# Softmax q/k group norm and short convolution placed inside the first input projection

## The reference, cut to what matters

```python
h = rmsnorm(x, attn_norm_w[l])
proj = h @ w_in[l]                     # 1024 -> 3072 columns
(q_a, k_a, v_a, q_b, k_b, v_b, g_b, g_c, x_c) = jnp.split(proj, split_points, axis=-1)
y_sb = from_heads(stick_breaking_attention(to_heads(q_a), to_heads(k_a), to_heads(v_a)))
qh = rmsnorm(to_heads(q_b), q_norm_w[l])   # per head of 64 features
kh = rmsnorm(to_heads(k_b), k_norm_w[l])
y_ch = from_heads(chunked_relpos_attention(qh, kh, to_heads(v_b), rel_bias[l]))
y_cv = short_conv_mixer(g_b, g_c, x_c, conv_w[l])  # gate * causal conv of width 3
y = group_rmsnorm(jnp.concatenate([y_sb, y_ch, y_cv], axis=-1), out_norm_w[l])
x = x + y @ w_out[l]
```

## Time and profile before

| | |
|---|---|
| device time, median of 3 runs | 2940.41 us (2938.57 to 2943.82) |
| device time of the profiled execution | 2938.94 us |
| its span in the trace | 2937.1 us |
| TensorE busy | 2767.3 us, 94% of the span |
| VectorE busy | 1657.0 us, 56% |
| GpSimd busy | 1157.6 us, 39% |
| ScalarE busy | 841.9 us, 29% |
| mean granted TensorE clock | 0.977 of full speed |

### The profile page before, as it was taken

One profiled execution on the slowest core, in us unless ns is written; L12 is line 12 of the kernel. 1 busy time (PEld: TensorE's weight loads), 2 busy tenths in 40 slices (PEclk: granted clock), 3 DMA queues, 4 the chain that ended last, 5 costly groups with the idle time before them and its releaser, 6 DMA issues.

```text
span 2937.1 us, 38574 instructions
## 1 busy us (share of the span) xinstructions
PE 2767.3 (94%) x13164; PEld 2188.6 (75%) x13164; DVE 1657.0 (56%) x3297; ACT 841.9 (29%) x1285; POOL 1157.6 (39%) x976
## 2 busy tenths in 40 slices
PE   6997899999999987999999999999999999999997
PEld 5863478878788764778777777888888888888775
DVE  4135642111599537469999956444444444444787
ACT  1133323322222427123445521222222222222111
POOL 4410155555455430453410044444444444444442
PEclk9988999999999999999999999999999999999998
DMA  4210033323223220222346764443443443443442
GB/s 141 88 36 22 15 94 95 98 93 100 87 93 94 78 88 28 65 89 79 94 151 236 253 196 140 114 129 113 115 129 110 119 128 109 120 124 112 128 129 64
DMA packets 208200, 315.44 MB, mean 107 GB/s; under 512 B 139888, under 2 KB 142320, under 8 KB 203888
## 3 DMA queue, kind: packets, MB, share of 16 engines
q1 hardware_dynamic: 63792, 233.34, 25.5%
q10 hardware_dynamic: 144320, 80.94, 10.0%
HBM read 275.45 MB, written 38.80 MB: 107 GB/s over the span
## 4 chain that ended last, share of the span: by engine, by line
PE 43%; issue 23%; DVE 18%; POOL 14%; ACT 1%; DMA 0%; DVEq 0%; ACTq 0%; POOLq 0%
POOL lo L431 14%; PE bank L1247 14%; PE bank L1248 14%; PE bank L1249 14%; DVE ohg L1173 3%; DVE bank L1200 1%; DVE oh L1169 1%; DVE oh L1170 1%; DVE WH L1202 1%; DVE lo L1181 1%; DVE eq L1146 1%; DVE idx L1088 1%; DVE idx L1080 1%; DVE scb L1081 1%; PE bank L1364 1%
## 5 line engine op out<-in xcount | busy, mean ns | idle before, releaser
L431 POOL TENSOR_TENSOR lo<-raw,hi 128x256 fp32r<-128x256 f32 (+1 forms) x972 | 1157.4, 1218 | 1741.5 <-ACT hi L457 911.9
L1247 PE MATMUL bank<-inH,hi 128*128 128x512 f32 x2240 | 893.9, 399 | 28.4 <-DVE inL L798 15.9
L1248 PE MATMUL bank<-inL,hi 128*128 128x512 f32 x2240 | 879.9, 393 | 0.0
L1249 PE MATMUL bank<-inH,lo 128*128 128x512 f32 x2240 | 879.6, 393 | 0.0
L1208 DVE TENSOR_TENSOR xT<-xT,bank 128x512 f32<-128x512 f32 x504 | 339.6, 685 | 538.4 <-PE bank L1249 538.4
L1247 PEld LDWEIGHTS bank<-inH,hi 128*128 128x128 f32 x2240 | 425.6, 190 | 125.9 <-issue 32.9
L1249 PEld LDWEIGHTS bank<-inH,lo 128*128 128x128 f32 x2240 | 425.0, 190 | 90.7
L1248 PEld LDWEIGHTS bank<-inL,hi 128*128 128x128 f32 x2240 | 426.2, 190 | 88.1 <-issue 2.2
L1247 PE MATMUL bank<-WH,hi 128*128 128x512 f32 x1024 | 408.5, 399 | 14.9 <-DVE xT L1208 14.9
L1248 PE MATMUL bank<-WL,hi 128*128 128x512 f32 x1024 | 404.0, 395 | 0.0
L1249 PE MATMUL bank<-WH,lo 128*128 128x512 f32 x1024 | 400.5, 391 | 0.0
(11 more groups left out here) (205 smaller groups left out, 2430.3 us busy)
## 6 DMA issues: line engine op xcount, KB each, us to landing
raw<-stream SPq DMA_DIRECT2D x440, 512.0 KB, 3.6
Gd<-gates ACTq DMA_DIRECT2D x32, 1024.0 KB, 7.4
gates<-stage_a ACTq DMA_DIRECT2D x16, 1024.0 KB, 4.3
gates<-stage_b ACTq DMA_DIRECT2D x16, 1024.0 KB, 4.2
tbl<-gqa ACTq DMA_DIRECT2D x8, 384.0 KB, 3.3
spilled<-res ACTq DMA_DIRECT2D x12, 256.0 KB, 3.1
A<-spilled ACTq DMA_DIRECT2D x6, 512.0 KB, 3.7
xT<-x SPq DMA_DIRECT2D x1, 2048.0 KB, 8.8
```

Of the source, the lines that this page charges most:

```text
L431: ins = pool.tensor_tensor(lo[:, r, part], raw[:, r, part], hi[:, r, part].bitcast(F32), ALU.subtract)
L1247: pe.matmul(bank, wh, xh, start=start, stop=False)
L1248: pe.matmul(bank, wh, xl, start=False, stop=False)
L1249: return pe.matmul(bank, wl, xh, start=False, stop=stop_)
```

## The change: what it does, and the diff

The norm of q_b and k_b and the convolution move ahead of stick-breaking attention, into the 24 tiles of the projection. VectorE squares tile m right after it took tile m out of its bank (m = 4 to 11). TensorE makes the sum of tile m-6 after tile m (m = 6 to 13); its loop over tiles 4 to 15 is written out for that. ScalarE takes the root in its turn of tile 15, and its loop is written out too. VectorE's reciprocal follows its copy of tile 15. TensorE spreads the first two tiles' roots after tile 17 and the other six after the first and third token group of each value pair (t = 0 and t = 2). VectorE's multiplications and the two halves of the convolution stand around its copies of the value tiles. Softmax attention then follows stick-breaking attention directly; ScalarE starts the loads of `tbl1b` right after its last copy there.

```diff
 # ScalarE
-            with act.Fori(1, N_IN // RING) as i:
-                for r in range(RING):
-                    high(S_IN, i, r + AHEAD)
+            for m in range(RING, N_IN):
+                if m == ROOT_TILE:
+                    group_root(n_sums + KD)
+                    n_sums += KD
+                high(S_IN, 0, m + AHEAD)
...
-            group_root(n_sums + KD)
-            n_sums += KD
             table(stage1, 1)
             attention(stage1)
 # VectorE
+            for m in range(18):
+                evacuate(m)
+                if 4 <= m < 12:
+                    square_qk(m - 4)
+                if m == ROOT_TILE:
+                    group_roots(n_root + 1)
+            put_qk(0)
+            put_qk(1)
+            dve.wait_ge(evac, T_IN + 18)
+            short_conv(0)
+            put_qk(2)
+            short_conv(1)
+            put_qk(3)
+            for m in (18, 20):
+                evacuate(m)
+                evacuate(m + 1)
+                put_qk(m // 2 * 2 - 14)
+                put_qk(m // 2 * 2 - 13)
             dve.wait_ge(spread_used, KD)
             dve.sem_inc(in_ready, 1)
+            evacuate(22)
+            evacuate(23)
 # TensorE
-            linear(S_IN, T_IN, 16, 1)
-            for m in (16, 17):
+            for m in range(RING, 18):
                 pe.wait_ge(evac, m - RING + 1)
                 pe.wait_ge(lo_done, m + 1)
                 tile(m % RING, B[m % RING][:, :])
+                if 0 <= m - SUM_LAG < KD:
+                    group_sum(n_sq, m - SUM_LAG)
+            n_sq += KD
+            n_rt += 1
+            pe.wait_ge(recips, n_rt)
+            spread_group(0, 0)
+            spread_group(1, 0)
             for m in range(18, N_IN, 2):
-                tiles_by_token(S_IN, T_IN, m)
+                tiles_by_token(S_IN, T_IN, m, lambda part: spread_group(m - 16 + part, 0))
+            pe.wait_ge(in_ready, 2)
...
             pe.wait_ge(y_sb, 2)
-            n_rt += 1
-            group_norm(n_sq, n_rt, 0, KD)
-            n_sq += KD
-            pe.wait_ge(in_ready, 2)
             attention(stage1)
```

More of the change, by code:

```diff
@@ L110 @@
 N_GRPS = D // HD
+SUM_LAG = 6
+ROOT_TILE = SUM_LAG + KD + 1
 PARTS = 2
@@ L831, in over_root, with group_roots @@
                 dve.reciprocal(rr[:, :width], rr[:, :width]).then_inc(recips, 1)
+            def group_roots(nth_root):
+                dve.wait_ge(roots, nth_root)
+                dve.reciprocal(rt[:N_GRPS, 0, :], rt[:N_GRPS, 0, :]).then_inc(recips, 1)
             def group_norm(src, put, n, nth_root, n_spread):
                 square_sums(src, n)
-                dve.wait_ge(roots, nth_root)
-                dve.reciprocal(rt[:N_GRPS, 0, :], rt[:N_GRPS, 0, :]).then_inc(recips, 1)
+                group_roots(nth_root)
                 for k in range(KD):
@@ L894, in _, with evacuate @@
             n_root += 1
-            for m in range(N_IN):
+            def evacuate(m):
                 dve.wait_ge(slot_used, S_IN + m + 1)
@@ L904, in _, with square_qk, put_qk, short_conv @@
                     take(m, dve.tensor_copy(by_token(v1, m, m - 18), bank[:, :].rearrange("p (t c) -> p t c", t=2)))
+            def square_qk(k):
+                dve.wait_ge(evac, T_IN + 4 + k + 1)
+                if k >= 2:
+                    dve.wait_ge(sums, n_sums + k - 1)
+                dve.tensor_tensor(sq[:, k % 2, :], qk1[:, 4 + k, :], qk1[:, 4 + k, :], ALU.mult).then_inc(squares, 1)
+            def put_qk(k):
+                dve.wait_ge(spread, n_spread + k + 1)
+                t = qk1[:, 4 + k, :]
+                dve.scalar_tensor_tensor(t, t, gain("qn" if k < 4 else "kn"), B[5 + k % 2][:, :], ALU.mult, ALU.mult).then_inc(spread_used, 1)
+            def short_conv(m):
+                gb, gc, xc = cv1[:, m, :], cv1[:, 2 + m, :], cv1[:, 4 + m, :]
+                tap = [gain("conv", 3 * m + j) for j in range(3)]
+                chain(dve.tensor_tensor(gc, gc, xc, ALU.mult))
+                chain(dve.tensor_scalar(xc, gc, tap[2], None, ALU.mult))
+                chain(dve.scalar_tensor_tensor(xc[:, 1:], gc[:, :T - 1], tap[1], xc[:, 1:], ALU.mult, ALU.add))
+                chain(dve.scalar_tensor_tensor(xc[:, 2:], gc[:, :T - 2], tap[0], xc[:, 2:], ALU.mult, ALU.add))
+                chain(dve.tensor_tensor(y1[:, 6 + m, :], xc, gb, ALU.mult))
+            chain(dve.tensor_scalar(gain("qn"), gain("qn"), QSCALE, None, ALU.mult))
+            for m in range(18):
[16 more added lines that the diff above has]
+                put_qk(m // 2 * 2 - 13)
+            dve.wait_ge(spread_used, KD)
+            dve.sem_inc(in_ready, 1)
+            evacuate(22)
+            evacuate(23)
+            n_spread += KD
+            n_sums += KD
+            n_root += 1
             dve.wait_ge(evac, T_OUT)
@@ L923, in _ @@
                     dve.tensor_tensor(mz[:, n % 2, :P], B[4 + n % 2][:, :P], neg, ALU.add).then_inc(s_masked, 1)
[L925 to L944, removed]
             attention(stage1)
@@ L1255, in tile, with tiles_by_token @@
                 m.then_inc(signal, 1)
-            def tiles_by_token(s0, t0, m):
+            def tiles_by_token(s0, t0, m, between=None):
                 r = m % RING
@@ L1268, in tiles_by_token @@
                         mm = mm3(out_cols, inH[:, k, tok], inL[:, k, tok], hi[:, r:r + 2, c], lo[:, r:r + 2, c], k == 0, k == KD - 1)
+                    if between and t % 2 == 0:
+                        between(t // 2)
                 mm.then_inc(slot_used, 2)
@@ L1325, in group_norm @@
                 for k in range(KD):
-                    pe.wait_ge(squares, n + k + 1)
-                    c = N_GRPS - 2 - 2 * k
-                    pe.matmul(B[4][:N_GRPS, :], halves[:, c:c + N_GRPS], sq[:, k % 2, :], start=k == 0, stop=k == KD - 1).then_inc(sums, 1)
+                    group_sum(n, k)
                 pe.wait_ge(recips, nth)
@@ L1331, in group_norm, with group_sum @@
                     spread_group(k, used)
+            def group_sum(n, k):
+                pe.wait_ge(squares, n + k + 1)
+                c = N_GRPS - 2 - 2 * k
+                pe.matmul(B[4][:N_GRPS, :], halves[:, c:c + N_GRPS], sq[:, k % 2, :], start=k == 0, stop=k == KD - 1).then_inc(sums, 1)
             def spread_group(k, used):
```

## The result

The changed kernel takes 2928.25 us (median of 5 runs, 2922.56 to 2929.43) against 2940.41 before (5 runs, 2938.57 to 2946.56). The ratio is 0.995 with a 95% interval of 0.9936 to 0.9964, so it is 10.6 to 18.8 us faster. On another chip it gave 2927.77 against 2938.90, ratio 0.9959 (0.9946 to 0.9973). Forecast were 2924 and 2917 to 2931: right in sign, mechanism and range, and 4 us too far down. The profiled execution took 2928.60 us, its span is 2926.8.

What follows compares the result with a forecast made beforehand. TensorE bounds the projection, a latency chain the stretch between the attentions. Added 8.4 + 9.6 = 18.0 us, removed 32.9 + 0.5 = 33.4, net -15.4: 2923.5 from the profiled 2938.94, 2925.0 by the median; forecast 2924, range 2917 to 2931.

Steps and rivals of the forecast that it cites:

- TensorE bounds the projection, a chain bounds what lies between the attentions: Projection: TensorE busy 116.00 of 116.00 us; between the attentions, 33 us of squares, sums, root, reciprocal and spreads in turn.
- What goes: 32.9 us: Between the attentions: scores start at 234.90 instead of 267.77, right after ScalarE's last copy of y, so 32.9 us go.
- Eight sums: 8.4 us, bounds 7.0 to 9.8: Projection, TensorE: each inserted sum adds 1.05 us, between 0.88 and 1.23, so eight add 8.4 us.
- the middle of 0.88 and 1.23: Price of one sum, 1.05 us, between a later norm's mean (0.88) and a spread with tile shape change (1.23).
- that case: Sums in the projection drain TensorE and cost like spreads: 9.8 us for eight, result 2924.9.
- Eight spreads: 9.6 us: Projection, TensorE: six alone between token groups at 1.23 us, two back to back after tile 17 for 2.2, together 9.6.
- the old chain's 1.67 us: Between the attentions a spread took 13.33 / 8 = 1.67 us; rival: all 16 insertions cost that, 2932 us, chance 0.05.
- TensorE waits for nothing, VectorE's work costs nothing: Projection: reciprocal ready with 6.8 us to spare; VectorE's 21.8 us of moved work lie beside TensorE, zero on the path.
- Clock: 0.5 us gained in softmax attention: Softmax attention starts behind faster-clocked stick-breaking, so its first stretch wins back 0.5 us (0 to 1.7).
- a stretch at half clock falls elsewhere: Rival: a 7.4 us stretch goes missing (2916, chance 0.09) or a second comes in stick-breaking or softmax attention (2931, 0.10).
- The slow rival: Softmax attention runs at half clock throughout, 51 us becoming about 87, +36, 2960 at worst; chance 0.03.

Runs made afterwards that it cites:

- the last pair: Changed kernel and kernel before, both with extra matmuls ahead of stick-breaking and at norms, the latter also between the attentions: 2916.52 and 2924.57 us.

## Why the prediction was right, point by point

- *TensorE bounds the projection, a chain bounds what lies between the attentions.* Right for the projection, which had no idle time after the change either. For the rest right in part: 3.5 of the 32.9 us were clock that 36 useless matmuls won back.
- *What goes: 32.9 us.* Right to 0.1 us in the profiled pair (33.53 - 0.65 = 32.88). Nothing was late in its place: the second table's memset stood 7.1 us after the first score, and what reads the table waited for that memset alone.
- *Eight sums: 8.4 us, bounds 7.0 to 9.8.* Measured 9.5. The mis-sized term was the price of one sum: I took the middle of 0.88 and 1.23, and it was 1.19. The experiment with 128 columns brings it to 0.90. So here the Trainium skill's rule on draining at a change of tiling mode ("TensorEngine Tiling (Array Packing)", "Tiling Modes") should have been taken whole: that case gave 9.8 us. That TensorE drains is its explanation; the runs show the price, 0.3 us a sum, and that it goes with the shape.
- *Eight spreads: 9.6 us.* Measured 9.2. The reason given for leaving the old chain's 1.67 us aside, a round trip with VectorE, was wrong: TensorE had no gap there, and 1.71 us a tile is its pace at half clock against 0.97 at full (the run with useless matmuls in the kernel before). The projection runs at full clock, so the choice of 1.23 was right all the same.
- *TensorE waits for nothing, VectorE's work costs nothing.* Right: TensorE was busy 135.92 of 136 us, and the reciprocal held nobody up.
- *Clock: 0.5 us gained in softmax attention.* Wrong in sign: 0.8 us lost there. I looked at its first part alone, which did gain 0.3; the last one lost 0.9, with the same 10.2 us at half clock in all.
- *What the parts make in the total.* -14.2 us by measured terms, -12.2 by the medians of the first set, -11.1 by the second. The forecast of -15.4 was 3 to 4 us too optimistic. The terms make 1.2 of that: 1.1 too little for the sums, 0.4 too much for the spreads, 0.5 of clock that was not won. The other 2 to 3 lie in parts that the change does not touch. The rival "a stretch at half clock falls elsewhere" was the right mechanism. Its price of 7.4 us holds for all of head 0, which took 10.31 us in the kernel before with the extra matmuls instead of 17.66; what came were several smaller stretches, and they should have been a term and not an alternative with a chance of 0.10. In the traces those parts go with the half clock: 122.5 and 119.4 us in two executions of the changed kernel, 116.2 outside the removed stretch before, and stage by stage as under the ledger. Why a stretch falls where it does is not shown. Nor is it proven that this is all of the missing 2 us in the medians, as the last pair has 1.6 us in the second block that the half clock does not explain. The range of 14 us was wide enough to hold all this; that the total fell within it says little about the clock.
- *The slow rival*, softmax attention at half clock throughout, did not come: its mean clock is 0.90 in both.

## What to carry to other kernels

Work taken out of a latency chain and put on a full engine is worth the chain minus the insertions, and both can be read in the profile of before, if the insertion is priced from a row with the same neighbours and the same tile shape. Give inserted matmuls the shape of their neighbours, even where most columns are wasted: 0.3 us each came back. And before moving work to save a few us, look at the granted clock behind each short idle time of TensorE; a few useless matmuls in those waits gave the kernel before more than the change did. With single executions 8 us and more apart, a change of a few us has to be judged in the timeline of its stage, and the total by many runs on one chip.

## What the runs showed of the hardware that I had not expected

- Extra matmuls in idle time alone made the kernel before some 18 us faster (2924.57 against 2944.53 on the same chip, ratio 0.9938, so 14 to 22 us).
- In the spreads of 16 rows and 64 columns the granted clock fell to 0.50 in the middle of 11.5 us of unbroken work, with 3.94 us of dense matmuls right ahead of them and 0.27 us of idle time between.
- A wait of 4 us on the path, with useless matmuls in it, left the total where the changed kernel's was (ratios to before 0.9955 and 0.9959); without them it cost 8.0 us.
- The same program, unedited, ran 2936.4 to 2948.2 us on one chip, and its mean granted clock went from 0.978 to 0.973 with it.
